# A hybrid decoder layer on one core: state scan on VectorE, sample products in column quarters, turned inputs loaded by SyncE, gate products dealt out among value steps

## What is computed

```
h = x + 1/2 * SwiGLU(RMSNorm(x))                                    (macaron half-step FFN 1)
n = RMSNorm(h); P = n @ w_in, with columns split into
    [u_s5 | q | k | v | q_idx | k_idx | w_idx | gate_s5 | gate_att]
branch S5 : complex-diagonal SSM over 32 groups of 16 channels with 64 states per group,
            y = Re(C s_t) + D u_t, then GELU and a GLU to D_MODEL
branch DSA: indexer I[t,s] = sum_h w[t,h] relu(q_idx[t,h].k_idx[s]); causal top-k;
            softmax attention over the chosen keys with a T5 bias, then projection to D_MODEL
h = h + (sigmoid(gate_s5) * S5 + sigmoid(gate_att) * DSA) @ w_out
h = h + 1/2 * SwiGLU(RMSNorm(h))                                    (macaron half-step FFN 2)
```

## Time and profile before

| | |
|---|---|
| median of 3 runs | 1506.16 us (1504.95 to 1506.29) |
| the profiled execution | 1504.8 us, span 1503.1 us, granted TensorE clock 0.979 |
| PE busy | 1425.5 us, 95% of the span |
| DVE, ACT, POOL busy | 609.4, 451.4 and 262.3 us |

### The profile page before, as it was taken

One profiled execution on the slowest core, in us unless ns is written; L12 is line 12 of the kernel. 1 busy time (PEld: TensorE's weight loads), 2 busy tenths in 40 slices (PEclk: granted clock), 3 DMA queues, 4 the chain that ended last, 5 costly groups with the idle time before them and its releaser, 6 DMA issues. The chain is left out here.

```text
span 1503.1 us, 27575 instructions
## 1 busy us (share of the span) xinstructions
PE 1425.5 (95%) x10734; PEld 1294.4 (86%) x10734; DVE 609.4 (41%) x957; ACT 451.4 (30%) x647; POOL 262.3 (17%) x458
## 2 busy tenths in 40 slices
PE   6999999999999989989999897989999999999996
PEld 5999999999977767767777774848999999999996
DVE  4333233434452267506666321205543443344344
ACT  4332222222330320145555331202332212221234
POOL 4000000487002109701134313110000000000000
PEclk8999999999998999999999999999999999999998
DMA  8522332232222472153211658661233223322221
GB/s 135 153 84 77 87 89 84 85 90 86 63 56 34 99 115 60 24 137 75 57 57 57 196 179 300 195 224 42 84 88 94 85 84 87 95 85 84 83 71 60
DMA packets 228746, 148.05 MB, mean 98 GB/s; under 512 B 29729, under 2 KB 211817, under 8 KB 228666
## 3 DMA queue, kind: packets, MB, share of 16 engines
q1 hardware_dynamic: 195904, 118.06, 27.1%
q0 software_dynamic: 7088, 19.65, 5.3%
q10 hardware_dynamic: 25674, 9.25, 3.4%
HBM read 139.62 MB, written 6.12 MB: 97 GB/s over the span
## 5 line engine op out<-in xcount | busy, mean ns | idle before, releaser
L1614 DVE TENSOR_TENSOR w_low<-wraw,w_high 128x1024 fp32r<-128x1024 f32 x144 | 180.4, 1254 | 318.8 <-ACT w_high L1141 318.8
L575 PE MATMUL ps<-hn_high,w_high 128*128 128x272 f32 x1408 | 292.4, 289 | 2.9 <-DVE w_low L1614 2.9
L575 PE MATMUL ps<-hn_high,w_low 128*128 128x272 f32 x1408 | 292.4, 289 | 0.0
L575 PE MATMUL ps<-hn_low,w_high 128*128 128x272 f32 x1408 | 291.3, 288 | 0.0
L1141 ACT ACTIVATE w_high<-wraw 128x1024 fp32r<-128x1024 f32 x144 | 152.5, 1060 | 443.0 <-PE ps L575 437.9
L575 PEld LDWEIGHTS ps<-hn_high,w_high 128*128 128x128 f32 x1408 | 222.4, 189 | 3.1 <-issue 3.0
L575 PEld LDWEIGHTS ps<-hn_low,w_high 128*128 128x128 f32 x1408 | 222.2, 189 | 0.0
L575 PEld LDWEIGHTS ps<-hn_high,w_low 128*128 128x128 f32 x1408 | 220.7, 190 | 0.0
L575 PE MATMUL ps<-act_high,w_high 128*128 128x272 f32 x832 | 173.1, 289 | 3.0 <-DVE act_low L1614 1.8
L575 PE MATMUL ps<-act_high,w_low 128*128 128x272 f32 x832 | 172.2, 288 | 0.0
L575 PE MATMUL ps<-act_low,w_high 128*128 128x272 f32 x832 | 171.6, 288 | 0.0
(11 more groups left out here) (328 smaller groups left out, 1591.8 us busy)
## 6 DMA issues: line engine op xcount, KB each, us to landing
wraw<-in_w_ffn_in SPq DMA_DIRECT2D x88, 512.0 KB, 3.9
wraw<-in_w_ffn_out SPq DMA_DIRECT2D x32, 512.0 KB, 4.0
wslot<-in_w_in SPq DMA_DIRECT2D x16, 512.0 KB, 4.0
wraw<-in_w_ffn_out SPq DMA_DIRECT2D x16, 384.0 KB, 3.4
wslot<-in_w_in SPq DMA_DIRECT2D x4, 1024.0 KB, 6.4
wslot<-in_cache_k POOLq DMA_DIRECT2D x16, 256.0 KB, 4.6
wslot<-in_w_s_glu SPq DMA_DIRECT2D x16, 256.0 KB, 3.1
wslot<-in_cache_k SPq DMA_DIRECT2D x16, 256.0 KB, 4.4
```

The source lines that it names most:

```text
L575: ins = pe.matmul(ps[:, bank + h, 0:HALF], a[:, w_at, k, :], x[:, lo_at(k) if x is x_lo else k, h * HALF:(h + 1) * HALF], start=(k == 0 an ...
L1614: return dve.tensor_tensor(o, a, b, op)
```

## The change

1. **Scan.** The same `advance` calls, word for word, stand in DVE's program instead of POOL's, behind the indexer sums and ahead of all selection.
2. **Selection.** Blocks 1 and 2 are selected right behind the scan (and behind `rbexp`); block 3 is only masked there. Its 16 rounds are made inside the loop of 32 steps, one in each step x below 24 with x % 3 < 2, behind the samples' round; its mask follows at x = 22. To allow this `sc[3]` lies in the memory of `ki4` (so DVE waits for `kidx_out` at x = 16), and `qbd` is filled later, behind the page copies.
3. **Column quarters.** `sample_cols` replaces the sample products of the index tile and the four kv tiles: 32 products of 64 streamed columns, each on its own 32 columns of the array (`tile_position`), instead of 8 of 256. The results lie on 128 partitions, so four small copies replace one on DVE and on ACT.
4. **Turned inputs.** SP, not ACT, issues the twelve `uch` transfers, behind the loads of q tiles 0 and 1 and ahead of those of q tiles 2 and 3. The store of the indexer keys moves ahead of q too.
5. **Chunk inputs** run with h inside c.
6. **Gate halves.** After key step 4 one, after the last key step two as before, after value steps 1 to 5 one each.
7. Pages of key steps 1 and 2 wait for POOL's mask counts 28 and 32 instead of DVE's 32; the final states' turn goes through `sg`, and the first glu sigmoid waits until they are stored.

```diff
-        GA_AFTER_K, GA_AFTER_V = (2, 3, 5, 6), (4, 5)
+        GA_AFTER_K, GA_AFTER_V = (4,), (1, 2, 3, 4, 5)
...
-                        eng.wait_ge(s["scores_biased"], 32)
                         for r in (1, 2):
+                            eng.wait_ge(s["tbm_done"], 24 + 4 * r)
...
             load("u", (0, rows("w_in"), C_U, P))
-            load("q", (0, rows("w_in"), C_Q, P))
-            load("kv", (0, rows("w_in"), C_K, 256))
-
             sp.wait_ge(s["evac"], EV0 + first_tile["u"])
...
+            load("q", (0, rows("w_in"), C_Q, P), hi=1)
+            sp.wait_ge(s["u_out"], 16 * 8)
+            sp.wait_ge(s["u_zero"], 1)
+            for k in range(CH):
+                sp.dma_start(uch[16 * k:16 * k + 16, :, 0:NC], scr_u[k].rearrange("q (g c) n -> c (q g) n", c=GC)).then_inc(s["u_in"], 16)
+            for k in range(NS):
+                sp.dma_start(uch[64 + 16 * k:80 + 16 * k, :, NC:UC], scr_us[k].rearrange("q (g c) n -> c (q g) n", c=GC)).then_inc(s["u_in"], 16)
+            load("q", (0, rows("w_in"), C_Q, P), lo=1)
+            load("kv", (0, rows("w_in"), C_K, 256))
...
+            def sample_cols(bank, cols_of):
+
+                for k in range(DK):
+                    for c in range(4):
+                        ins = pe.matmul(ps[32 * c:32 * c + 32, bank, 0:64], hn[:, k, SEQ:NT], cols_of(k, c), start=(k == 0), stop=(k == DK - 1),
+                                        skip_group_check=True, tile_position=(0, 32 * c))
+                return ins
...
-                acc(ps[0:32, b + 3, 0:256], [(hn[:, k, SEQ:NT], w[:, k, 0:256]) for k in range(DK)])
+                sample_cols(b + 3, lambda k, c: w[:, k, 64 * c:64 * c + 64])
...
-                    for h in range(2):
-                        for c in range(2):
+                    for c in range(2):
+                        for h in range(2):
...
+                sample_cols(4 * slot + 2, lambda k, c: w[:, k, 64 * c:64 * c + 64]).then_inc(s["mm_done"], 1)
...
-                ga_half(8 * g + 4)
-                ga_half(8 * g + 5)
-                pe.wait_ge(s["ga_ev"], 8 * g + 6)
+                ga_half(8 * g + GA_K)
+                ga_half(8 * g + GA_K + 1)
+                pe.wait_ge(s["ga_ev"], 8 * g + GA_K + 2)
...
-                act_e.activation(dst[0:32, 4, c0:c0 + 256], ps[0:32, 4 * half + 2, 0:256], ACT.Copy).then_inc(s["evac"], 1)
+                for c in range(4):
+                    ins = act_e.activation(dst[0:32, 4, c0 + 64 * c:c0 + 64 * c + 64], ps[32 * c:32 * c + 32, 4 * half + 2, 0:64], ACT.Copy)
+                ins.then_inc(s["evac"], 1)
...
+            def select(qb):
+                dve.tensor_scalar(selq[qb], sc[qb], 0.5 * TAKEN, MASK, ALU.is_ge, ALU.mult).then_inc(s["prompt_selected"], 1)
+                dve.wait_ge(s["prompt_selected"], qb)
+            for qb in range(1, 4):
+                w = P * (qb + 1)
+                link(tt(sc[qb][:, w - P:w], sc[qb][:, w - P:w], caus[:], ALU.add))
+                if qb < 3:
+                    top(sc[qb], TOPK_P // 8)
+                    select(qb)
...
+                    top_round(scs)
+                    if x < 24 and x % 3 < 2:
+                        top_round(sc[3])
+                    if x == 22:
+                        select(3)
```

More of the change, by code:

```diff
@@ L1080, in _ @@
                     if i in GA_AFTER_V:
[L1081 removed]
+                        ga_half(8 * g + GA_K + 2 + GA_AFTER_V.index(i))
             pe.wait_ge(s["sample_values_out"], 2)
@@ L1435, in _ @@
                 act_e.activation(ptS[0:32, 8, :], ps[0:32, 5, 0:P], ACT.Copy).then_inc(s["sample_probs_out"], 1)
-                ga_out(8 * g + 6)
-                ga_out(8 * g + 7)
+                for m in range(len(GA_AFTER_V)):
+                    ga_out(8 * g + GA_K + 2 + m)
             act_e.wait_ge(s["sample_att_turned"], 1)
@@ L1534, in _ @@
             pool.memset(uch[0:64, :, NC:UC], 0.0).then_inc(s["u_zero"], 1)
[L1537 to L1556, removed]
@@ L1849, in _ @@
                 dve.wait_ge(s["relu_done"], x + 1)
+                if x == 16:
+                    dve.wait_ge(s["kidx_out"], 32)
                 if h == 0:
@@ L1856, in _ @@
             dve.wait_ge(s["index_added"], 24)
-            for qb in range(1, 4):
-                w = P * (qb + 1)
-                link(tt(sc[qb][:, w - P:w], sc[qb][:, w - P:w], caus[:], ALU.add))
-                top(sc[qb], TOPK_P // 8)
-                dve.tensor_scalar(selq[qb], sc[qb], 0.5 * TAKEN, MASK, ALU.is_ge, ALU.mult).then_inc(s["prompt_selected"], 1)
-                dve.wait_ge(s["prompt_selected"], qb)
-            dve.wait_ge(s["evac"], EV0 + first_tile["kv"])
-            link(dve.memset(qbd[:].rearrange("p j b r -> p (j b r)"), 0.0))
@@ L1867, in _, with advance @@
-            for j in range(4):
-                for h in range(2):
-                    sl = slice(64 * h, 64 * h + 64)
-                    hh = 2 * j + h
-                    ins = dve.tensor_copy(qbd[sl, j, :, NS * hh:NS * hh + NS], qT[sl, j, SEQ:NT].rearrange("p (b q) -> p b q", b=NB))
-            link(ins)
+            def advance(dst, src, a, shape):
+                w = int(np.prod(shape))
+                tm = [prodmem[:, w * k:w * (k + 1)] for k in range(4)]
+                if len(shape) == 2:
+                    tm = [x.rearrange("p (a b) -> p a b", a=shape[0]) for x in tm]
+                link(tt(tm[0], src[0], a[0], ALU.mult), tt(tm[1], src[1], a[1], ALU.mult),
+                     tt(tm[2], src[0], a[1], ALU.mult), tt(tm[3], src[1], a[0], ALU.mult))
+                link(tt(tm[0], tm[0], tm[1], ALU.subtract), tt(tm[2], tm[2], tm[3], ALU.add))
+                link(tt(dst[0], dst[0], tm[0], ALU.add), tt(dst[1], dst[1], tm[2], ALU.add))
@@ new lines, in _ @@
+            dve.wait_ge(s["chunk_inputs_out"], 4)
+            link(dve.memset(vst[:, :, :, 0:1], 0.0))
+            vb = vst[:, :, :, 1:1 + NC].rearrange("p c g (b j) -> p c g b j", j=8)
+            for j in range(1, 8):
+                advance([vb[:, c, :, :, j] for c in range(2)], [vb[:, c, :, :, j - 1] for c in range(2)],
+                        [cpow[:, 1, c, :].unsqueeze(2).broadcast_to([P, GP, 8]) for c in range(2)], (GP, 8))
+            for b_ in range(1, 8):
+                advance([vb[:, c, :, b_, 7] for c in range(2)], [vb[:, c, :, b_ - 1, 7] for c in range(2)],
+                        [cpow[:, 8, c, :] for c in range(2)], (GP,))
@@ new lines, in _ @@
+            for j in range(7):
+                advance([vb[:, c, :, 1:8, j] for c in range(2)], [vb[:, c, :, 0:7, 7] for c in range(2)],
+                        [cpow[:, j + 1, c, :].unsqueeze(2).broadcast_to([P, GP, 7]) for c in range(2)], (GP, 7))
+            link(*[dve.tensor_copy(fin_s[:, c, :, :], vst[:, c, :, 1 + NC:1 + UC].rearrange("p g b -> p b g")) for c in range(2)],
+                 *[dve.tensor_copy(fin_p[:, c, :], vst[:, c, :, NC]) for c in range(2)])
+            advance([fin_s[:, c] for c in range(2)], [s0[:, c] for c in range(2)],
+                    [apow[:, 4, c, :].unsqueeze(1).broadcast_to([P, NB, GP]) for c in range(2)], (NB, GP))
@@ L1888, in _ @@
                 dve.tensor_copy(kxT[:, both % 2, :], ps[:, 4, :]).then_inc(s["pages_out"], 1)
+            dve.wait_ge(s["evac"], EV0 + first_tile["kv"])
+            link(dve.memset(qbd[:].rearrange("p j b r -> p (j b r)"), 0.0))
+            for j in range(4):
+                for h in range(2):
+                    sl = slice(64 * h, 64 * h + 64)
+                    hh = 2 * j + h
+                    ins = dve.tensor_copy(qbd[sl, j, :, NS * hh:NS * hh + NS], qT[sl, j, SEQ:NT].rearrange("p (b q) -> p b q", b=NB))
+            link(ins)
             dve.wait_ge(s["sample_index"], 2)
```

62 lines of the change are left out of this document (21 added, 41 removed).

## The result

The changed kernel takes **1497.32 us** (median of five, 1493.93 to 1498.55) against 1506.16 before: ratio 0.9942, 95% interval 0.9931 to 0.9953. It is 8.8 us faster where 24.2 were forecast, and outside the range of 1474 to 1495. The same kernel measured again (e9) gave 0.9935 [0.9922, 0.9948].

What follows compares the result with a forecast made beforehand. PE, busy 95% of the span, was taken as the bound, so only its program or waits count. 1504.8 - 12.2 (to the page turn) - 12.0 (gate halves) = 1480.6 profiled, 1482.0 for the median; range 1474 to 1495.

Steps and rivals of the forecast that it cites:

- Column quarters: Sample parts of kv and index tiles: 1.0 us each, 2.6 saved a tile, -10.4 us for four kv tiles.
- rival E: Sample parts: small matmuls start no faster than twice 13 ns, 1.6 us a part; 1484 us in all, chance 0.15.
- Index tile -2.3: Index tile's sample part: quarters save 2.6 us, less three more DVE copies under 0.11 us each.
- ACT's three more copies: +0.3: Behind the last kv tile: ACT's extra small copies of the sample part add 0.3 us to PE's path.
- Turned inputs: Before kv: PE waits 3.4 us ahead of q tile 2 instead of 5.09 later; reorder alone worth 0.9 us.
- Its rival: Turned inputs before q tile 2: SP issues them faster, so PE's wait there is 0; no chance given.
- DVE's scan "36.8 us": Scan moved to DVE before the page turns: 36.8 us, from 557.9 to 594.7, ends 33 and 50.
- rival A: First page turn: scan up to 50 us makes DVE late, turn waits up to 13 us longer; 1492, chance 0.14.
- three ends: First page turn: PE's path 648.1, DVE's selection 648.9, SP's pages 649.2; the last sets it, -12.2 us.
- The loop: Loop of 32 steps: block 3's rounds on DVE fit its idle time, cost 0; ends 0 and +5.
- Gate halves "-12.0": Sample attention's two groups: value-stage waits vanish, key steps lose cover; net -12.0 us, ends -7 and -14.
- the slow clock behind it: Value stages of the sample attention: half-clock losses of 0.97 and 1.74 us a group vanish with the 5.13 us wait.

Runs made afterwards that it cites:

- e9: The changed kernel itself measured again, nothing changed against it; ratio 0.9935 to the kernel before.
- e4: Changed kernel with the kv tiles' sample parts wide as before (16 products of 256 columns); 1497.4 us, ratio 0.9959 to the kernel before.
- e5: Changed kernel with sample quarters first in each kv tile and ACT copying them while the wide products run; ratio 0.9996 to the kernel before.
- e11: e5 plus a wait on ACT that puts its bias-row loads behind the indexer pages; ratio 0.9940 to the kernel before.
- e13: e4 with ACT's copy of the wide sample part cut into four pieces of 64 columns; ratio 0.9957 to the kernel before.
- e16: e4 with ACT's copy of the wide sample part cut into eight pieces of 32 columns; ratio 0.9979 to the kernel before.
- e17: Changed kernel with the scan on POOL again, as before the change, second measurement; ratio 0.9924 to the kernel before.
- e6: Changed kernel with real and imaginary parts of the scan joined, five instructions a step instead of eight; ratio 0.9911 to the kernel before.
- e1: Kernel before with only the new table of gate halves; 1501.6 us, ratio 0.9971 to the kernel before.

## Why the prediction was wrong

- **Column quarters, right on PE.** The sample parts take 1.10 us for 1.0; 64 matmuls in 1.03 us are 16 ns each. The rule of the Trainium skill, "TensorE: Matmul & The Clock Gate" (section "Wait — 56ns, not 53.3ns?"), of some 25 ns at least did not hold for these matmuls on four column groups in turn, and rival E with it.
- **"Index tile -2.3" was wrong: -0.3.** PE reaches the lag kernels 2.6 us earlier, but their second half waits for DVE, 2.31 us for 1.72. DVE's four copies of the sample queries take 1.70 us where one took 1.20, and I had priced them at under 0.11 each without following the chain that waits for them. Behind the longer wait the clock falls, and the second half takes 5.34 us for 3.67. The rows are DVE's copies and PE's second half, before and after. Of the 17 traces with the quartered index tile 12 show this, 14.3 us from the lag kernels to u tile 0; five have 12.6; the two with the wide tile have 12.0.

```profile
474.59 1.20 DVE L1817 COPY sg<-ps 32x1024 f32<-32x1024 f32 x1
477.45 3.67 PE L750 MATMUL ps<-biasmem,qkT 64*16 64x128 f32 x64 [1.72 <-DVE big L1826]
...
472.00 1.70 DVE L1788 COPY sg<-ps 32x256 f32<-32x256 f32 x4
475.45 5.34 PE L766 MATMUL ps<-biasmem,qkT 64*16 64x128 f32 x64 [2.31 <-DVE big L1798]
```

- **"ACT's three more copies: +0.3" was the costliest error on PE's own path.** They cost 0.55 us: the four, three of them from other partitions, take 0.88 us, e13's four on the same partitions 0.52, and the one before took 0.36. This brought PE's wait from 1.37 to 1.92, behind which the clock falls: +4.1 between key turns and head weights. Shown by e4, e5, e11, e13 and e16. The rows are of ACT, changed kernel and e13.

```profile
620.67 0.88 ACT L1327 ACTIVATE kvtok<-ps 32x64 f32<-32x64 f32 x4
...
630.07 0.52 ACT L1328 ACTIVATE kvtok<-ps 32x64 f32<-32x64 f32 x4
```

- **Turned inputs, right as far as one trace can say.** A wait of 2.39 us for 3.4, slow clock of 1.7 behind it, chunk inputs at full clock: kv begins at 559.2 for 558.2: of the index tile's missing 2 us this shorter wait gave one back. Its rival (no wait, as SP issues faster) and the order of the chunk inputs had no run of their own.
- **DVE's scan "36.8 us" took 44.** The rows I interpolated were contiguous; these are strided. The step of 128 columns takes 0.31 us a product here and 0.225 in the unstrided one (0.90 for four); the last two sums of a call, strided too, take 0.34 each where the contiguous two before them take 0.245. I had bounds of 33 to 50 and took the low side. The scan also began 1.2 us later, but in my sum the constants held the selection until 598, so DVE ended at 654.7 instead of 648.9, 5.8 us late, as much as the page turn. That was rival A, at 6 us instead of up to 13. SP's pages ended at 650.9 instead of 647.5.
- **But no one of the three ends was to be had alone.** By e17 and e6, taking DVE's error away moves the turn by 1 us, since PE's own path had become late by its own 5 us. Had PE come at 648, as forecast, with SP's pages issued until 650.9, as measured, it would have met the collision of e5, which no rival held: I priced ACT's bias rows nowhere.
- **The loop, right:** DVE's extra rounds cost nothing. From the loop's first scores to group 0 it is 166.8 us before and 166.7 after, and 166.7 to 167.0 in all 19 traces; what differs between page turn and group 0 (184.9 to 191.8) lies ahead of the loop.
- **Gate halves "-12.0" gave -5.0, the largest miss.** The removed waits (9.7 us in two groups) were right, and so were the added ones: page turns wait 8.0 us for DVE instead of 5.1, 2.9 more for the 3.0 forecast. The term that failed is "the slow clock behind it": I booked 2.7 us of loss a group to it as gone. But 10.2 us at half clock appear at the start of group 1 instead, and 3.4 behind it, a loss of some 6. e1, with the table alone, has 6.8 us at half clock at the start of group 1 too, and a rest of 501.2 for 497.9.

The sign was right and the gain too high. Of the 24.2 us forecast 11.1 came in the profiled execution: 7.0 are missing at the gate halves, 5.9 up to the page turn and 0.2 between. Two steps failed. In the sum of PE's program, each term that ends or shortens work was booked as if the clock stayed full behind it, and none of the new waits lowered it elsewhere; that cost some 6 us in and behind the groups and 4.1 behind kv. At the page turn DVE's scan was mis-sized, 44 us for 36.8. Either alone would have held the turn within about 1 us of where it came. The other 2.3 us, from 11.1 to the medians' 8.8, are nearly all that the changed kernel's fastest execution was traced.

## What to carry to other kernels

A wait removed from PE doesn't always remove the slow clock with it; look at PE's next waits too, short ones included, as a few tenths of a us of ACT's or DVE's work inside one can cost several times as much (0.55 us of copies behind kv, 4.1 us on PE). Price small copies that replace a large one wherever PE waits for them. Where three ends meet within a few us, price all three, and ask which transfers an earlier engine will start: an issue that comes 4 us sooner can stand in front of another queue's last small loads. Take durations for strided operands from strided rows.

## What was not expected of the hardware

- Which waits are followed by half clock differs between traces of kernels that are the same up to there: the lag kernels' second half took 3.67 us in five traces and longer in twelve. The changed kernel itself had 6.8 us at half clock around the page turn in one trace and 10.2 in the other. That this makes most of the spread of one kernel's times is argued, not shown: one trace stands for each measurement.
- Behind kv 0.21 us more of PE's waiting (1.53 to 1.74) parts a full clock from 6.8 us at half. It is no rule for other places: in the lag kernels waits of 1.72 to 2.07 us left the clock full (seven traces), those of 2.18 to 2.32 did not (twelve). The Trainium skill, "TensorE: Matmul & The Clock Gate" (section "A second HAM failure mode: psum-queue depth-cycling"), tells of another kernel whose clock goes down and up where PE idles briefly but often; the stretch behind kv, with no long wait, agrees with it.
- Loads of 16 KB that land 1.8 us after issue took up to 13.7 us beside eight loads of 256 KB from another queue (e5).
